# The prompt's four linear-attention output-projection halves, spread between the row turns and router products of the sample tiles

## The reference, cut to what matters

```python
def encoder_layer(x, ...):
    h = rms_norm(x, norm1_g)
    gq, gk, gv, gog, glr_f, glr_b, dq, dk, dv = jnp.split(h @ w_in, offs, axis=-1)
    a = gla_mixer(...)                 # gated linear attention, 512 columns
    d = diff_attention(...)            # differential attention, 512 columns
    x = x + concatenate([a, d]) @ w_out      # w_out is 1024 x 1024
    h2 = rms_norm(x, norm2_g)
    x = x + expert_choice_ffn(h2, w_router, w_gate, w_up, w_down)
    return x

def expert_choice_ffn(h, ...):         # 16 experts
    aff = softmax(xt @ w_router)       # 16 columns
    gates, idx = lax.top_k(aff.T, cap) # 64 sample and 32 prompt tokens for each expert
    ...                                # gather rows, SwiGLU with 1024 x 2048 weights, scatter-add
```

## Time and profile before

| what | value |
|---|---|
| median of the three runs | 1530.77 us |
| profiled execution: span | 1529.8 us |
| profiled execution: the device time outside its span | not shown; the median is 0.97 us above the span |
| PE busy | 1501.1 us (98%) |
| DVE busy | 1247.9 us (82%) |
| ACT busy | 1091.5 us (71%) |
| chain that ended last, share of PE | 90% |

### The profile page before, as it was taken

How to read it: one execution, slowest core, us unless ns; L and a number is a source line. 1 busy time by engine, 2 the same in 40 slices (tenths; PEclk the granted TensorE clock), 3 DMA queues, 4 the chain that set the end, 5 groups by cost and what they waited for, 6 DMA issues and landing times.

```text
span 1529.8 us, 18639 instructions
## 1 busy us (share of the span) xinstructions
PE 1501.1 (98%) x7271; PEld 1229.4 (80%) x7271; DVE 1247.9 (82%) x1151; ACT 1091.5 (71%) x1231; POOL 169.4 (11%) x123
## 2 busy tenths in 40 slices
PE   7999999999999999999999999999999999999997
PEld 7787777677878888888888888888888888888886
DVE  4348689775688898888989888888989888898985
ACT  7555456875357878787787878778787877778774
POOL 1013131000020201010110101011010101101010
PEclk9999999999899999999999999999999999999999
DMA  6111103202669999999999999999999999999993
GB/s 234 56 55 56 55 2 110 99 1 88 257 234 386 382 381 373 395 376 393 374 387 385 373 394 376 393 375 388 382 377 389 377 394 376 394 376 387 393 378 112
DMA packets 192246, 447.98 MB, mean 293 GB/s; under 512 B 13272, under 2 KB 13600, under 8 KB 192160
## 3 DMA queue, kind: packets, MB, share of 16 engines
q1 hardware_dynamic: 187776, 434.08, 76.3%
q0 software_dynamic: 4224, 12.65, 3.6%
q10 hardware_dynamic: 160, 0.07, 0.0%
HBM read 434.19 MB, written 12.58 MB: 292 GB/s over the span
## 4 chain that ended last, share of the span: by engine, by line
PE 90%; DVE 6%; ACT 2%; issue 1%; DMA 0%; POOL 0%; POOLq 0%; DVEq 0%; ACTq 0%
PE ps L992 23%; PE ps L994 23%; PE ps L993 23%; PE ps L655 5%; PE ps L656 4%; PE ps L657 4%; PE ps L1027 1%; DVE states L1549 1%; PE ps L881 1%; PE ps L913 1%; PE ps L972 1%; PE ps L985 1%; PE ps L926 1%; DVE slice_low L1457 1%; PE ps L897 1%
## 5 line engine op out<-in xcount | busy, mean ns | idle before, releaser
L1917 DVE TENSOR_TENSOR wl<-raw,wh 128x2048 fp32r<-128x2048 f32 x384 | 873.2, 2290 | 126.1 <-ACT wh L1397 124.4
L1397 ACT CAST wh<-raw 128x2048 fp32r<-128x2048 f32 x384 | 731.9, 1915 | 124.2 <-PE ps L994 122.8
L992 PE MATMUL ps<-wh,XTh 128*128 128x512 f32 x1024 | 404.9, 395 | 0.9 <-issue 0.9
L994 PE MATMUL ps<-wl,XTh 128*128 128x512 f32 x1024 | 399.5, 390 | 0.0
L993 PE MATMUL ps<-wh,XTl 128*128 128x512 f32 x1024 | 398.5, 389 | 0.0
L994 PEld LDWEIGHTS ps<-wl,XTh 128*128 128x128 f32 x1024 | 192.2, 188 | 41.2
L992 PEld LDWEIGHTS ps<-wh,XTh 128*128 128x128 f32 x1024 | 192.3, 188 | 38.9 <-issue 1.1
L993 PEld LDWEIGHTS ps<-wh,XTl 128*128 128x128 f32 x1024 | 192.5, 188 | 38.1
L992 PE MATMUL ps<-wh,gTh 128*128 128x512 f32 x512 | 200.9, 392 | 0.0
L994 PE MATMUL ps<-wl,gTh 128*128 128x512 f32 x512 | 199.5, 390 | 0.0
L993 PE MATMUL ps<-wh,gTl 128*128 128x512 f32 x512 | 199.2, 389 | 0.0
(11 more groups left out here) (248 smaller groups left out, 1606.6 us busy)
## 6 DMA issues: line engine op xcount, KB each, us to landing
raw<-in_w_gate SPq DMA_DIRECT2D x128, 1024.0 KB, 11.2
raw<-in_w_up SPq DMA_DIRECT2D x128, 1024.0 KB, 11.5
raw<-in_w_down SPq DMA_DIRECT2D x128, 1024.0 KB, 12.0
slice_raw<-in_w_in SPq DMA_DIRECT2D x5, 2048.0 KB, 8.0
X<-in_x_sample SPq DMA_DIRECT2D x8, 512.0 KB, 6.9
slice_raw<-in_w_out SPq DMA_DIRECT2D x2, 2048.0 KB, 8.0
X<-in_x_prompt SPq DMA_DIRECT2D x4, 512.0 KB, 7.0
slice_raw<-in_w_in SPq DMA_DIRECT2D x4, 512.0 KB, 7.6
```

What stands on the lines that cost most here:

```text
L992: pe.matmul(out, hi, rhs_h, start=first, stop=False)
L994: return pe.matmul(out, hi, rhs_l, start=False, stop=last)
L1397: act.copy(wh[:, n % CONV, :], raw[:, n % RAW, :]).then_inc(s_wh, 1)
L1917: dve.tensor_tensor(wl[:, n % CONV, :], raw[:, n % RAW, :], wh[:, n % CONV, :].bitcast(F32), ALU.subtract).then_inc(s_wl, 1)
```

## The change

The gla halves (0,0), (0,1) and (1,0) move in PE's list, with the waits of the banks 5 and 6. The fourth, (1,1), keeps its place. No instruction is added or removed, and no other engine's list changes.

```diff
             pe.wait_ge(s_wtc, len(ATT))
-            gla_half(0, 0, LAST_BANK[0, 0], None)
             rows_turned(3)
             pe.wait_ge(*fill_read(last_in_bank(7)))
             router_logits(2)
+            gla_half(0, 0, LAST_BANK[0, 0], None)
             rows_turned(4)
             router_logits(3)
+            pe.wait_ge(s_pvc, len(ATT))
+            gla_half(0, 1, LAST_BANK[0, 1], None)
             rows_turned(5)
             router_logits(4)
-            pe.wait_ge(s_pvc, len(ATT))
-            gla_half(0, 1, LAST_BANK[0, 1], None)
+            pe.wait_ge(*fill_read(last_in_bank(6)))
+            gla_half(1, 0, LAST_BANK[1, 0], None)
             router_logits(5)
             diff_turned(0)
-            pe.wait_ge(*fill_read(last_in_bank(6)))
-            gla_half(1, 0, LAST_BANK[1, 0], None)
             pe.wait_ge(s_aff, 1)
```

## The result

| | before | after |
|---|---|---|
| median | 1530.43 us (18 runs, 1527.4 to 1532.38) | 1532.88 us (18 runs, 1530.59 to 1535.2) |
| span of the profiled execution | 1529.8 us | 1531.2 us |

The change made the kernel slower: by 2.45 us between the medians, ratio 1.0017 with a 95% interval of 1.001 to 1.0023. The forecast was 1.9 us faster. The time lies inside the range, near its upper end, and the sign is wrong. The difference is under the 0.3% that the prediction took for what a measurement can hardly tell from none, but the interval over 18 runs a side leaves 1 out.

A forecast was written before the change was run, and what follows sets the result against it. PE was taken to bound the kernel, busy 98% of the span. Work of 18.23 us plus waits of 1.05 and 2.05 gave 21.33 against 23.20 us, 1.87 us earlier: 1528.9 us, range 1526.8 to 1533.2.

The forecast's parts named there:

- The new order, walked through at the full clock: PE from attention to the affinity transposes: 18.23 us of work plus two waits, 21.33 against 23.20 us, 1.87 us earlier.
- rival A: Clock falls at the new affinity wait, half (1,1) at 1.2 GHz, 2.03 us more: 1530.9 us; chance 0.17.
- rival B: Clock falls before half (0,0), after 6.9 us without a half, costing 4.97 us: 1533.9 us; chance 0.13.
- steps (1) and (6): PE idles 1.05 us before rows_turned(3), for ACT's copy, and 2.05 us before the affinity transposes, for DVE.
- A to T: From the end of attention to the start of the affinity transposes: forecast 21.33 us, against 23.20 before.
- steps (2) to (5): Turns 0.87 to 0.92, routers 1.69, halves 2.78 us at the full clock; router_logits(5) ends 1.14 us earlier.
- step (7): SyncE's store of DVE's hn row is issued 1.1 us later; taken as 0, bound 0 to 0.5 us of loss.
- Rival C: The fall before was that execution's own; most keep the clock, new order 0.7 us slower: 1531.5 us; chance 0.20.
- step (8): After the transposes all shifts by 1.87 us; filler 11.75 us; clock and first gather taken as 0, kept -1.3 to +2.6.

The follow-up runs named there:

- e4: The change plus useless 512-column matmuls in both of PE's gaps, 4 ahead of rows_turned(3) and 8 behind diff_turned(0): 1529.81 us, ratio to before 0.9994.
- e10: The change plus 4 useless 512-column matmuls in the first gap only, ahead of rows_turned(3): 1530.89 us, ratio to before 1.0007.
- e11: The change plus 8 useless 512-column matmuls in the second gap only, behind diff_turned(0): 1530.47 us, ratio to before 1.0006.
- e9: The kernel before, unchanged, run once more for a second trace: 1531.60 us, one run.
- e6: Against the kernel before, only half (0,1) moved, between router_logits(3) and rows_turned(5): 1527.78 us, ratio 0.9986.
- e8: The kernel before with nothing moved, plus 3 filler matmuls of 512 columns behind each of router_logits(2) and router_logits(3): 1527.59 us, ratio 0.998.
- e5: Against the kernel before, halves (0,0) and (0,1) each cut into two pieces of 6 matmuls, spread among turns and routers: 1527.68 us, ratio 0.9978.
- e7: e5 with DVE writing the normed rows of tiles 4 and 5 behind the sample's affinity chain: 1525.77 us, ratio to before 0.9967.

## Why the prediction was wrong

**The step that failed: "The new order, walked through at the full clock".** The walk-through took the full clock from 380 us on as the likeliest case (0.45), with its loss at the affinity wait as rival A (0.17) and ahead of half (0,0) as rival B (0.13). Both happened, in both traces of the change, and together, which no case of the prediction was. The price of the falls over the whole of the runs is 3.4 us (e4 against the change, each against before). Put in place of the 0 of the walk-through, it turns -1.87 into +1.6 us; 2.45 was measured. The rest is what the walk-through missed at the full clock too: e4, which kept it, came out 0.98 us faster than before, not 1.87. That the time still lies inside the range is luck. A and B together, at their stated prices, give 1535.9 us, outside it; in the first trace of the change the fall before half (0,0) cost 1.67 us, not 4.97, because the low clock lasted 3.4 us and not 10.2, and the one at half (1,1) 1.56, not 2.03.

**The waits, steps (1) and (6): right.** 1.05 and 2.05 us forecast, 1.19 and 2.00 measured, the same in both traces. Their sum over the full clock, A to T, was forecast at 21.33 us; e4, e10 and e11, which kept the clock, have 21.8.

**Half (1,0) and the routers, steps (2) to (5): right but for small terms.** Halves at the full clock 2.87 instead of 2.78 us.

**The store, step (7): 0 was right, for the change.** DVE's row of tile 5 started at 397.47 us without a wait. For the kernel before it was mis-sized. The prediction took the landing of one trace (397.23 us), with 1.1 us of slip at most. From the issue of the store to its landing, e9, e6 and e8 have 10.49, 9.60 and 7.59 us, and in the second trace of before this, not the clock, set the transposes. Rival C had that mechanism and put before at about 20.6 us from A to T; it was 22.2.

**Two readings behind the chances were wrong.** Against rival C the prediction held that the span of the profile is not above the runs. But every run that is on record with its span is about 1.8 us longer than it, so the profiled execution of 1529.8 us took about 1531.6, on the slow side of a median of 1530.43, and a typical run had less to win than its trace. The condition of rival C, that most executions keep the clock, does not hold by the mean clocks above: 60 of 78 runs lost as much as the traces with the early fall. Against rival B it counted eight 128-column products of attention between 376.95 and 380.21 us; the trace has twelve.

**The end, step (8): in its bounds, by another path.** The filler was 10.51 instead of 11.75 us, but PE then waited 0.86 us for the gather: the last normed prompt row's store took 5.43 us to land (5.32 in the second trace). So the floor from the gather, named as a stop for gains, took back 0.86 of the 1.24 us that the shorter filler gave.

**What the prediction overlooked** is the link between its own parts. It counted 3.10 us of new idle time as time only, and listed stretches without a half as risks only. But the order that uncovers a wait also strips PE of dense work around it, so that in both traces each new wait came with a fall of the clock, on the half behind it. It is the lack of dense work that the runs point to, more than the wait itself: the early falls of the old order and that of e6 came with PE busy, and fillers, which are dense work, kept the clock in both orders. The evidence was in its own text: the two new stretches were 6.9 and 4.4 us long, the one that lost the clock before 4.5. The Trainium skill, "TensorE: Matmul & The Clock Gate", Part 4, on transposes not counting as busy like other matmuls, spoke against the change. Both traces of the change agree with it as far as they go: the clock fell 2.4 us behind the first wait, after a turn and within the 16-column products, and 0.6 us behind the second, after transposes and within the half; no trace here can put it down to the transposes alone. In hindsight the weight of 0.30 for A and B together was too small.

What stays open: how often each single fall occurs in each kernel. The mean clocks of the runs tell how much was lost in all, not where; three traces of before and two of the change are too few for that, and no experiment fixed when the clock may change.

## What to carry to other kernels

Before dense work is moved to fill one thin stretch, look at what it hides where it stands: the first and the last piece of a fill often cover a latency, and moved away they leave a wait and a low clock behind it, which here cost about as much again as the wait. Move only the pieces in the middle (e6: one of three, 2 to 3 us faster), or cut the pieces (e5), and then look at which engine the next wait names, here DVE behind a store (e7). When runs of a kernel spread more than a rival's, compare traces of several executions, and the mean clock of every run, before taking one for the rule. Holding the clock with a few useless matmuls in the waits is a cheap experiment that separates the cost of a wait from the cost of the clock.

## What the runs showed of the hardware that was not expected

Filler matmuls inside a wait paid here. Twelve of 512 columns (2.7 us of PE time in 3.2 us of gaps) won 3.4 us and drew the spread of eleven runs from 4.6 us down to 1.0. Six of them in the old order, 1.37 us of pure extra work in PE's list, made the kernel 3.4 us faster. And the landing of one 512 KB store in the same place of the chain differed from 7.6 to 10.5 us between kernels and executions where DVE waited for it. In the change, where it was issued later (390.77 us) and the row that needs it started without a wait at 397.47, it took at most 6.7.
